# Interleaving the first two column groups of five stages, moving side work, and another ending, in a one-core transformer kernel

## The reference

```python
# first block: two layers, x and a context of 256 tokens, modulated by a condition c
xm = x * (1 + scale_c) + shift_c
# layer 0: mLSTM with 4 heads in two directions, beside a multi-scale pool
q, k = silu(conv3(xm @ w_q)), silu(conv3(xm @ w_k))     # context: keys and values only matter
h    = mlstm_forward + mlstm_backward                   # gates: log_i, log_sigmoid(log_f)
x    = layer_norm(alpha * x + g_c * (y @ w_out_even))
# layer 1: spatial gating unit, then layer_norm again
x    = layer_norm(alpha * x + g_c * ((u * (w_sp @ layer_norm(v)) * silu(z)) @ w_out_odd))
# second block
ret, rnn = retention(8 heads), rg_lru(conv4(...))       # both from rmsnorm(x)
x = x + (merge of ret and rnn) @ w_mix_out
x = x + cross_attention(rmsnorm(x), mem, 4 heads) @ w_xa_o
x = x + (silu(gate) * val) @ w_ffn_down                 # d_ff 5632
out = rmsnorm(x) * final_norm_w                         # mean of squares over 2048, per token
```

## Time and profile before

| | us |
|---|---|
| timed, median of 3 | 3126.73 (3126.59 to 3126.88) |
| the profiled execution | 3128.8 |
| its span, first to last record | 3127.0 |
| mean granted clock of TensorE | 0.994 of full speed |

### The profile page before, as it was taken

How to read it: one execution, slowest core, us unless ns; L and a number is a source line. 1 busy time by engine, 2 the same in 40 slices (tenths; PEclk the granted TensorE clock), 3 DMA queues, 4 the chain that set the end, 5 groups by cost and what they waited for, 6 DMA issues and landing times.

```text
span 3127.0 us, 44871 instructions
## 1 busy us (share of the span) xinstructions
PE 3052.9 (98%) x16818; PEld 2612.5 (84%) x16818; DVE 2140.3 (68%) x2704; ACT 1572.9 (50%) x1929; POOL 51.7 (2%) x52
## 2 busy tenths in 40 slices
PE   7899999999999999999999999999999999999998
PEld 5688878888788887888888888888888888888887
DVE  3389878788587776646668865566457777777544
ACT  3355444456434566534556654445345555555443
POOL 0032000000000000000000000000000000000000
PEclk9999999999999999999999999999999999999999
DMA  9977848786578656655555555575345555555554
GB/s 391 369 244 256 286 168 306 274 318 199 182 242 295 238 182 195 203 167 184 186 182 169 182 187 190 180 245 187 122 161 181 189 188 188 188 191 191 189 188 141
DMA packets 180247, 666.41 MB, mean 213 GB/s; under 512 B 20084, under 2 KB 20468, under 8 KB 178808
## 3 DMA queue, kind: packets, MB, share of 16 engines
q1 hardware_dynamic: 178424, 660.09, 61.6%
q10 hardware_dynamic: 1664, 4.19, 0.3%
HBM read 657.91 MB, written 6.29 MB: 212 GB/s over the span
## 4 chain that ended last, share of the span: by engine, by line
PE 88%; DVE 5%; DMA 3%; ACT 2%; DVEq 1%; issue 1%; SPq 0%; ACTq 0%
PE acc L757 47%; PE acc L761 23%; PE acc L768 4%; PE acc L770 4%; PE acc L769 4%; DVE w_lo L2002 2%; DMA ada_more<-in_w_ada 1%; DMA mod_raw<-in_w_mod 1%; PE msc L811 1%; ACT w_hi L1286 1%; PE acc L942 1%; PE msc L888 1%; DMA raw<-in_w_xa_k 1%; DMA raw<-in_w_mix_out 0%; PE msc L1184 0%
## 5 line engine op out<-in xcount | busy, mean ns | idle before, releaser
L2002 DVE TENSOR_TENSOR w_lo<-raw,w_hi 128x1024 fp32r<-128x1024 f32 x1020 | 1241.5, 1227 | 635.7 <-ACT w_hi L1286 626.4
L1286 ACT CAST w_hi<-raw 128x1024 fp32r<-128x1024 f32 x1020 | 1061.5, 1048 | 866.5 <-PE acc L761 592.8
L757 PE MATMUL acc<-a_pair,w_hi 128*128 128x512 f32 x2944 | 931.5, 398 | 5.5 <-DVE a_pair L2911 2.4
L761 PEld LDWEIGHTS acc<-a_pair,w_lo 128*128 128x128 f32 x2944 | 554.1, 188 | 131.0
L757 PE MATMUL acc<-b_pair,w_hi 128*128 128x512 f32 x1792 | 570.9, 400 | 16.1 <-DVE w_lo L2002 16.1
L761 PE MATMUL acc<-a_pair,w_lo 128*128 128x256 f32 x2944 | 579.5, 278 | 0.0
L757 PEld LDWEIGHTS acc<-a_pair,w_hi 128*128 128x128 f32 x2944 | 451.2, 189 | 8.7 <-DVE a_pair L2911 2.8
L757 PE MATMUL acc<-f_pair,w_hi 128*128 128x512 f32 x1408 | 442.4, 395 | 0.0
L761 PEld LDWEIGHTS acc<-b_pair,w_lo 128*128 128x128 f32 x1792 | 337.8, 189 | 80.1
L761 PE MATMUL acc<-b_pair,w_lo 128*128 128x256 f32 x1792 | 353.2, 279 | 0.0
L761 PEld LDWEIGHTS acc<-f_pair,w_lo 128*128 128x128 f32 x1408 | 264.5, 188 | 62.5
(11 more groups left out here) (358 smaller groups left out, 2477.4 us busy)
## 6 DMA issues: line engine op xcount, KB each, us to landing
raw<-in_w_ffn_up SPq DMA_DIRECT2D x176, 512.0 KB, 4.1
mod_raw<-in_w_mod SPq DMA_DIRECT2D x128, 512.0 KB, 5.1
raw<-in_w_ffn_down SPq DMA_DIRECT2D x88, 512.0 KB, 3.3
ada_more<-in_w_ada SPq DMA_DIRECT2D x40, 512.0 KB, 14.4
raw<-in_w_xa_k SPq DMA_DIRECT2D x32, 512.0 KB, 12.6
raw<-in_w_k SPq DMA_DIRECT2D x32, 512.0 KB, 4.7
raw<-in_w_v SPq DMA_DIRECT2D x32, 512.0 KB, 5.0
raw<-in_w_even_out SPq DMA_DIRECT2D x32, 512.0 KB, 4.4
```

Of the source, the lines that this page charges most:

```text
L757: pe.matmul(acc[:, bank(stage, g) + m, :], w_h[:, cols], pair[:, :, kc, :], start=begin, stop=False, skip_group_check=True)
L761: mm = pe.matmul(acc[:, bank(stage, g) + m, 0:T], w_l[:, cols], pair[:, 0, kc, :], start=False, stop=end, skip_group_check=True)
L1286: nc.scalar.copy(w_hi[:, slot], source).then_inc(hi_done, 1)
L2002: vec.tensor_tensor(w_lo[:, slot], source, w_hi[:, slot].bitcast(F32), ALU.subtract).then_inc(lo_done, 1)
```

## The change

- **woven.** Five stages (ctx_k, sgu_v, ret_q, mix_out, xa_o) run the units of their first two groups alternately: (group 0, chunk block 0), (group 1, block 0), (group 0, block 1) and so on. In ctx_k the gate units thereby stand at units 7 and 8 rather than 4 and 5.
- **Places.** The 13 products of `MOD_AT` in lat_k, spread over 18 steps, become nine, in steps 9 to 17; the others go to lat_o, pool_u, mlstm_z and pool_z (one more each), and those of lat_q avoid its last two steps. `MASKED_AT` moves from 15 to 14, `MIX_AT` from (6, 9, ...) to (7, 10, ...), `TURN_AT` by two units, `head_at` by one.
- **sgu_v.** DVE keeps the two normalising products, at listed steps; the scale and shift that make buf_a go from DVE to ACT, and the other scale and shift on ACT go to steps 24 to 39.
- **mem_vb.** Normalise, squares, affine and quarter sums of each quarter stand two steps apart, and the tail runs on into ret_q.
- **The ending.** PE multiplies the last unit bank by bank; copy, additions and squares of that group are half as large and follow each bank. The squares of earlier groups go into one running block (one more DVE addition, 128x256, per group); PE adds the last two blocks of squares itself. ACT loads the root's table ahead of the last copy. The scaled output is made in eight pieces, with eight transfers.

```diff
-    Stage("ctx_k", "w_k", "F", 1, gate=True, act=1, dve=1),
+    Stage("ctx_k", "w_k", "F", 1, gate=True, act=1, dve=1, woven=True),
...
+        if woven:
+            first = self.kinds[:2 * group_units]
+            self.kinds[:2 * group_units] = sorted(first, key=lambda kind: (kind[2], kind[1]))
...
-MOD_AT = {"ctx_k": (13, 16), "ctx_v": spread(16, 9), "lat_k": spread(18, 13), "lat_v": spread(16, 9),
-          "lat_q": spread(16, 11), "lat_o": spread(16, 12), ...
+MOD_AT = {"ctx_k": (13, 16), "ctx_v": spread(16, 9), "lat_k": range(9, 18), "lat_v": spread(16, 9),
+          "lat_q": (0, 1, 2, 4, 5, 6, 8, 9, 10, 12, 13), "lat_o": spread(16, 13), ...
...
-    h, step = divmod(j - (DC // KU + 1), DC // KU)
+    h, step = divmod(j - (DC // KU + 2), DC // KU)
...
-            for q in range(4):
+            for q in range(8):
                 sp.wait_ge(dve_step, BEFORE["final"]["dve"] + q + 1)
-                nc.sync.dma_start(t["out"][:, 4 * q:4 * q + 4, :], y_out[:, 4 * q:4 * q + 4, :]).then_inc(y_stored, 16)
+                nc.sync.dma_start(t["out"][:, 2 * q:2 * q + 2, :], y_out[:, 2 * q:2 * q + 2, :]).then_inc(y_stored, 16)
...
+            def last_group(stage, g, n_used):
+                nc.scalar.activation(tiny[:, 0:1], tiny[:, 21:22], ACT.Sqrt)
+                act.wait_ge(acc_free, (stage.iters - 1) * stage.groups + (stage.g0 + g + 2))
+                act.wait_ge(first_bank_used, stage.iters * stage.groups)
+                nc.scalar.copy(halves_b[:, 0:1, :], low_part(stage, g)[:, 0:1, :]).then_inc(half_copied, 1)
+                act.wait_ge(unit_used, n_used)
+                nc.scalar.copy(halves_b[:, 1:2, :], low_part(stage, g)[:, 1:2, :]).then_inc(half_copied, 1)
...
-            def high_part(hi, q, name, after=None):
+            def high_part(hi, q, name, before=None):
                 steps.wait(dve=q + 1)
+                if before:
+                    for c in range(2):
+                        before(buf_a[:, 2 * (q % 2) + c, :], 2 * q + c)
+                    act.drain()
                 steps.done(nc.scalar.copy(hi[:, 2 * q:2 * q + 2, :], buf_a[:, 2 * (q % 2):2 * (q % 2) + 2, :]))
-                if after:
-                    after(2 * q)
-                    after(2 * q + 1)
```

More of the change, by code:

```diff
@@ L126 @@
     Stage("mem_va", "w_xa_v", "T", 1, groups=1),
-    Stage("sgu_v", "w_sgu_v", "T", 1, groups=4, act=1),
+    Stage("sgu_v", "w_sgu_v", "T", 1, groups=4, act=1, woven=True),
     Stage("sgu_u", "w_sgu_u", "F", 1, groups=4, act=0, dve=1),
@@ L749, in run @@
                         w_l = w_lo[:, slot].rearrange("p a b -> p (a b)")
+                        if stage is LAST and last:
+                            for m in range(2):
+                                for c in range(chunks):
+                                    kc = chunks * k + c
+                                    cols = slice(c * 2 * P + m * P, c * 2 * P + (m + 1) * P)
+                                    pe.matmul(acc[:, bank(stage, g) + m, :], w_h[:, cols], pair[:, :, kc, :], start=False,
+                                              stop=False, skip_group_check=True)
+                                    mm = pe.matmul(acc[:, bank(stage, g) + m, 0:T], w_l[:, cols], pair[:, 0, kc, :], start=False,
+                                                   stop=(c == chunks - 1), skip_group_check=True)
+                                mm.then_inc(unit_used if m else first_bank_used, 1)
+                            continue
                         for c in range(chunks):
@@ L1304, in finish @@
                 def finish(i, g, n_used):
+                    if stage is LAST and i == stage.iters - 1 and g == stage.groups - 1:
+                        return last_group(stage, g, n_used)
                     act.wait_ge(unit_used, n_used)
@@ L1707, in _, with both_affines @@
             run("even_out", with_squares(modulated(0)), side=mem_again(a_hi, 2, "pool_z"))
+            def both_affines(out, c):
+                return nc.scalar.activation(out, x[:, c, :], ACT.Identity, bias=both_affine[:, 1, c:c + 1],
+                                            scale=both_affine[:, 0, c:c + 1])
             def sgu_chunks(j):
@@ L1762, in mix_chunks @@
                     steps.done(mm)
+                q = MIX_X_AT.get(j)
+                if q is not None:
                     act.drain()
@@ L1778, in halves @@
                 dve.add()
-            run("ret_q", lambda i, g: halves(qf, g))
+            run("ret_q", lambda i, g: halves(qf, g), side=lambda j: mix_chunks(STAGE["mem_vb"].n + j))
             run("ret_k", lambda i, g: halves(kf, g))
@@ L1949, in weighted @@
                     mm = nc.scalar.activation(y_out[:, c, :], x[:, c, :], ACT.Copy, scale=col("final_norm", c))
-                ran(mm)
+                return mm
             run("ffn_down", squares_and_weighted, by_half=True)
-            rms("final")
-            weighted(DC - 2)
+            steps.wait(pe=1)
+            steps.done(nc.scalar.activation(spare[:], msc[:, 0, 0:T], ACT.Sqrt, bias=tiny[:, 21:22], scale=1.0 / D))
+            steps.done(weighted(DC - 2))
+            steps.end("final")
         @block.gpsimd
@@ L2064, in finish @@
                         return then
+                    if stage is LAST and i == stage.iters - 1 and g == stage.groups - 1:
+                        return last_group(stage, g)
                     out = dest(i, g) if dest else buf_a[:, 2 * (g % 2):2 * (g % 2) + 2, :]
@@ L2138, in pair_step @@
                     dve.drain()
[L2139 to L2143, removed]
+                    steps.done(make(q))
                 if q == 9:
@@ L2147, in rms_of, with make @@
             def rms_of(slab, weight):
[L2148 to L2154, removed]
-                                             mod[:, 48 * layer + c, which:which + 1], ALU.mult, ALU.add)
+                def make(q):
+                    for c in range(2 * q, 2 * q + 2):
+                        mm = vec.scalar_tensor_tensor(buf_a[:, 2 * (q % 2) + c % 2, :], slab[:, c, :], col(weight, c), rstd[:],
+                                                      ALU.mult, ALU.mult)
+                    return mm
                 return make
@@ L2732, in rotated @@
                 return group
-            run("ret_q", rotated(qf), dest=in_slab(qf))
+            run("ret_q", rotated(qf), side=lambda j: mix_chunks(STAGE["mem_vb"].n + j), dest=in_slab(qf))
             run("ret_k", rotated(kf), dest=in_slab(kf))
@@ L2976, in _ @@
             reciprocal_of_root(1)
-            dve.wait_ge(act_done, ACT_DONE["ffn_down"])
-            for q in range(4):
-                part = y_out[:, 4 * q:4 * q + 4, :]
-                steps.done(vec.tensor_tensor(part, part, bcast(rstd, 4), ALU.mult))
+            for q in range(8):
+                if q == 0:
+                    dve.wait_ge(act_done, ACT_DONE["ffn_down"])
+                if q == 7:
+                    steps.wait(act=2)
+                part = y_out[:, 2 * q:2 * q + 2, :]
+                steps.done(vec.tensor_tensor(part, part, bcast(rstd, 2), ALU.mult))
             steps.end("final")
```

84 lines of the change are left out of this document (53 added, 31 removed).

## The result

The changed kernel takes 3109.57 us (median of five, 3108.23 to 3113.28) against 3126.73 before (five runs, 3126.23 to 3127.11): ratio 0.9948, 95% interval 0.9936 to 0.9961. The forecast was 3109.1. The profiled execution has a span of 3106.4 us and is the fastest of the five (3108.23); before's was 2.1 us above its median, so the two spans differ by 20.6 us and the medians by 17.2. Two executions on record, one of the kernel with four output transfers (6634.83 us) and one of the kernel before beside it (4101.35 us), lie far outside all others and are left out of the medians, ranges and ratios.

A forecast was written before the change was run, and what follows sets the result against it. PE, busy 98% of the span, was taken as the bound, with some 30 us of its waits for DVE open to change. Stage terms summed to -17.6 us, taken off the 3126.7 median: 3109.1, own range 3103 to 3115, 8-in-10 range 3097 to 3122.

The forecast's parts named there:

- lat_k, sgu_u: PE's waits for gates (3.1 of 3.9 us) and mixing (2.4) go with the slow-clock stretches behind them: -5.7 and -4.0.
- lat_q: The 4.6 us wait for the last state stays; two products leaving the last steps are replaced by ones with late transfers: +0.5.
- The end: Half-size last-group work saves 1.3 us before the output products; an earlier first transfer and smaller pieces bring it to -2.0.
- ctx_k and ctx_v: New bank wait, gates back to back with convolution, one slow stretch, second convolution under POOL's run: +8.1, bounds +3 and +12.
- sgu_v: PE's 6.7 us of waits for b_pair fall to 3.2, a 6.2 us chunk loop against two units of 5.7: -3.5.
- mem_vb: PE's 3.1 us of waits for w_lo shrink, but column sums wait for the moved last quarter: -0.5, bounds -4 and +3.
- Attention: Four waits for xa_qf (3.6 us together) and the 2.4 us wait for the last head's output chunks go: -6.0.
- A: Rival, chance 0.14: slow-clock stretches in lat_k, sgu_u and rnn_x stay or move to other waits, 5.9 us more, 3115.0.
- B: Rival, chance 0.16: ctx_k's lead of four units absorbs gates and convolution, so the 8.1 us loss vanishes, 3101.0.
- C: Rival, chance 0.12: sgu_v, ret_q, mix_out and xa_o also wait for freed banks; 3126 with one wait per stage, 3143 with two.
- D: Rival, chance 0.05: eight output transfers each take as long as the four did, overlapping no further than two; +4.8, 3114.
- E: Rival, chance 0.05: removed waits reappear one unit later at DVE's next late work; only -4.5 in all, 3122.2.

The follow-up runs named there:

- the mended kernel: Changed kernel with ctx_k not woven, attention reload in eight pieces, mem_vb's column sums one step later, three modulation products moved to other stages: 3092.71 us.
- the second experiment: Changed kernel with ctx_k not woven but its two gate units still at 7 and 8: 3107.30 us, ratio 0.9936.
- the first experiment: Changed kernel with ctx_k not woven, gate units at 4 and 5 again: 3104.97 us, ratio 0.9925.

## Why the prediction was right, and where its terms were off

The sum was right because the waits of PE were the right thing to add up, and each was traced to the work on DVE that stood ahead of it. That the median fell within half a microsecond of the forecast is luck beside that: stage by stage the two profiled executions differ by 20.5 us against the 17.6 of the sum, and the runs of the changed kernel spread over 5 us.

*lat_k, sgu_u:* mechanism and size hold, by an experiment each that puts the old places back. In sgu_u wait and stretch come back whole, in lat_k 3.0 of the 3.9 us and 4.0 of the stage's 5.8.

*lat_q:* the +0.5 was right in size (+0.7), the reason hardly. That late transfers hold up the products is true, and the mended kernel shows what it costs, but it was so before: there the same product waited 3.46 us, after the change 3.72. What is new is a split between the mask work and the last group's addition, for which DVE waits 2.11 us until ACT is done. First a row of before, then one of after:

```profile
420.28 1.23 DVE L2013 SCALAR_TENSOR_TENSOR mod_raw<-mod_raw,cond_wide 128x1024 f32<-128x1024 f32 x1 [3.46 <-DMA mod_raw<-in_w_mod]
```
```profile
428.64 1.23 DVE L2054 TENSOR_TENSOR w_lo<-raw,w_hi 128x1024 fp32r<-128x1024 f32 x1 [2.11 <-ACT w_hi L1308]
```

From the start of lat_q the late products come 0.2 us later than before and the addition 0.8. So by the trace the moved mask work was not free; no run puts it back alone.

*The end:* -2.0, measured -1.8. The parts were sized less well: up to the first output product -1.6 (forecast -1.3), behind it -0.2 (-0.7). The output products start 4.94 us after the last big product, not "some 4"; the forecast's own -1.3 off 6.5 would have been 5.2.

*ctx_k and ctx_v:* the term was +8.1, measured +5.7. In ctx_k the steps hold: the wait for the bank 2.52 (forecast 2.6), the wait for the split 3.75 ("some 3.5"), one slow stretch. What failed is the last step, that the second convolution under POOL costs PE 1.6: that convolution itself moved 5.4 us later, and POOL's run ends at 227.45, before its last part. DVE's timeline after the change:

```profile
226.71 1.81 DVE L2348 SCALAR_TENSOR_TENSOR buf_b<-buf_a,prm,buf_b 128x255 f32<-128x255 f32 x4
228.59 1.67 DVE L2352 SCALAR_TENSOR_TENSOR buf_b<-buf_a,prm,buf_b 128x255 f32<-128x255 f32 x4
```

Its last part takes the same 1.67 us as in the earlier trace rows, all three 5.22 against 4.96; PE, itself later, did not wait behind it, and ctx_v is 0.4 shorter than before. Of the two waits the forecast priced the bank at +1.4 and the gates with the stretch at 3.5 + 1.6 = 5.1; the second experiment shows 1.1 and 5.5.

*sgu_v:* -3.5, measured -4.8. The loop of about 6.2 us per chunk is there (6.18), and the waits left are smaller than the forecast's 3.2: 1.5 for b_pair and 0.67 at the first unit, which the view puts down to issue. The reason was half wrong. The prediction set the loop against two units and so counted on the woven order; the run without it has nearly the same gain. What made it was that DVE gave up an operation per chunk, and the loop of 6.2 is not a property of ACT having the work but of placing a chunk every second step.

*mem_vb:* -0.5, measured -2.0. PE's waits for w_lo shrank, from 2.6 to 0.7 (the other 0.5 of the 3.1 in the earlier trace rows lies in ctx_v). The wait for the column sums came as described, 2.9 where it was 1.9, but this profile had no slow stretch behind it, where before's had one. In six of nine profiles with this wait there was one, and it costs 1.6, so on the mean the gain is nearer to -0.9.

*rnn_x:* -4.5, measured -3.4: the wait for v_ret and its stretch are gone, but 61 us into the stage, behind the first turning, PE now waits 0.66 for a split. The prediction looked for nothing next there, and no run puts the old places of the turning back.

*Attention:* -6.0, measured -7.3. The five waits are gone; more came back than they were long. No run puts the old places back, so that the edits ended these waits is argued from the trace. Nor were the two edits taken apart: with the heads one unit later, xa_o not woven would have PE wait in unit 3 for output that the same PE makes only at unit 4. The 1.3 us stay open.

*mix_out and pool_u:* forecast 0, measured +1.5 and +0.8. In mix_out the old wait for a split whose weights come late, 1.64 before and 1.79 now, drew a slow stretch this time; with the reload in pieces wait and stretch go (89.2). The prediction said that nothing waits there. In pool_u a new wait of 0.5 for a split stands early in the stage. With the old places of the products it is gone (45.4). It is not the tenth product in pool_u alone: the mended kernel has nine there, but fourteen in lat_o, and waits 0.60. So the products added in lat_o, just ahead, are the likelier cause; no run takes them apart. The prediction gave neither a price.

*Rivals.* A, the clock not coming back, is refuted in lat_k, sgu_u and rnn_x, though mix_out drew a new stretch. B, ctx_k hiding its block, is refuted by the first experiment. C: no woven stage but ctx_k shows a wait for a freed bank. D: eight pieces end 0.3 us sooner than four. The Trainium skill's rule on batching ("DMA: Bandwidth & Descriptors", section "Bandwidth") does not decide here, where transfers overlap and the first one's start counts. The estimate of 2.6 us for 256 KB by the fit in its "Anatomy of one DMA", which that section gives for transfers issued by gpsimd, stands beside 2.4 measured here on SP's queue. E, gains eaten at the next thing, happened only as small change (0.66 in rnn_x, 0.5 in pool_u).

## What to carry to other kernels

Read the gain of moving side work from the wait it ends and look at what then stands next to what on the late engine: two long blocks with splits between them were free, the same two without them cost 5.5 us, the slow stretch included. A change of many parts is judged place by place: here one part lost 6.6 us beside the 17 that the whole gained, and only the time from stage to stage shows that. When a change helps, take its parts off one at a time before crediting the one with the best name, and try its places too: weaving sgu_v was worth 0.4 us at one set of steps and 3.3 at another.

## What the runs showed of the hardware

The same wait is followed by a stretch at 1.2 GHz in one execution and not in the next. The wait of 3.75 us in ctx_k drew one in all eight profiles that have it, the wait of 2.83 to 2.88 us in mem_vb in six of nine, the 2.5 us for the bank in three of seven. In mix_out the wait itself varied: the five of 1.79 to 2.46 us drew one, the five of 1.56 to 1.77 us (the kernel before among them) did not. That its length alone decides is ruled out by mem_vb, where 2.83 drew one and 2.87 did not. Two windows, first of mem_vb in the kernel with ctx_k not woven, then just behind the same wait in the changed kernel:

```profile
1184.40:1187.80 3.40, 3.20 (x8) 2.54 (x9) 2.42 (x3) 0.47 (x1) 0.00 (x0) 0.50 0.70 240
```
```profile
1190.00:1193.40 3.40, 3.40 (x16) 2.82 (x15) 1.92 (x2) 0.70 (x2) 0.00 (x0) 1.00 0.79 266
```

Such a stretch costs 1.5 to 1.7 us in ctx_k and mem_vb, some 1.1 in mix_out. With five such waits in the changed kernel this fits runs that spread by 5 us (3108.23 at a mean clock of 0.996, 3113.28 at 0.994). What decides it in one execution no run here shows.
